# A hybrid recurrent and convolution layer on one core: the order of work in the first chunk of the input projection

## The chip, the cores and the metric

The kernel runs on one core of a Trainium2 chip. The core has TensorE for matmuls (PE in the profile; its weight loads are PEld), VectorE (DVE), ScalarE (ACT), GpSimd (POOL) and SyncE (SP), which issues nearly all transfers here. The metric is the device time of one execution in microseconds (us).

## The reference

One decoder layer over 512 prompt tokens and 8 x 4 sample tokens. A combined projection gives four branches, which are mixed, projected, normalised and sent through a SwiGLU block. Cut to what bears on the change:

```python
z = x @ w_in                       # x: (tokens, 1024), w_in: (1024, 8192)
a_x, a_gate, b_val, b_gate, c_in, d_b, d_c, d_h, gates = jnp.split(z, ...)   # 8 parts of 512 columns, 4 x 1024 gates
a_conv = causal_dwconv(rg_buf, a_x, rg_conv_w)          # width 4, then the RG-LRU recurrence
glu = b_val * jax.nn.sigmoid(b_gate)
b_conv = causal_dwconv(cf_buf, glu, cf_conv_w)          # width 31, then LayerNorm and swish
y_c = pool_mixer(pool_buf, c_in, ...)                   # trailing means over 2/4/8/16 tokens, small matmuls
sc_conv = causal_dwconv(sc_buf, d_c * d_h, sc_conv_w)   # width 3: the "short conv"
y_d = d_b * sc_conv
merged = sum(jax.nn.sigmoid(gates[n]) * (branches[n] @ w_branch[n]))
x = layer_norm(ALPHA * x + merged @ w_out)
x = layer_norm(ALPHA * x + (silu(x @ w_ff_gate) * (x @ w_ff_up)) @ w_ff_down)
```

The outputs are the tokens and the last rows of every convolution buffer. All is float32, to float32 accuracy.

## The kernel before, in words

**Layout.** Activations stand transposed, channels on the 128 partitions and 544 tokens (512 prompt, 32 sample) along the free dimension. Every float32 operand is split into a high and a low part in the 32-bit format that TensorE takes at full rate, and a product is three matmuls: low weights by high x, high by low, high by high.

**Units.** Weights come in units of up to 8 x 128 x 128 elements, through a ring of four slots. For each unit SyncE issues the transfer (`raw`), ScalarE makes the high part (`hi`, line 669, to `w_hi`), GpSimd the low part (`lo`, line 528, to `w_lo`), and TensorE runs `unit` (line 1089): 8 chunks of x, three products, two halves of 272 tokens, so 48 matmuls or 24 pairs.

**The input projection.** It has four chunks of 128 channels (c = 0 to 3), each of 8 units in the order B_VAL, B_GATE, D_C, D_H, D_B, C_IN, A_X, A_GATE. They alternate between two PSUM slots (`main`), and `in_tile` (lines 697 and 1115) couples the engines by counts of emptied slots (`tile_out`). ScalarE empties most units. D_H is emptied by VectorE itself, which multiplies it by d_c into `dch_pad` (lines 1567 to 1570). This is the short-conv product, and unit 5 of a chunk, C_IN, can't start on TensorE before it is done, as both use the same slot.

**VectorE in a chunk** (from line 1548): it waits for `tails_taken`, a transpose of TensorE at the end of the chunk before; builds `glu_pad`; convolves the 32 sample tokens in three instructions (`conformer_steps`, lines 1526 to 1530); adds prompt taps 0 to 11 of the width-31 convolution (`conformer_taps`, line 1545, one instruction a tap); makes the short-conv product and its three taps, taps 12 to 15, y_d, taps 16 to 28, the width-4 convolution, the last taps and their sum (line 1600). In the last chunk `lambda_parts` prepares ScalarE's exp.

**The start.** TensorE transposes x (lines 1099 and 1108), runs unit 0, then transposes small vectors and states that came in 21 small transfers (lines 1126 to 1138, 17 transposes), then runs unit 1, then waits for the copies of these transposes out of PSUM (`misc_ready`, `tails_out`), sends a transpose that counts as `tails_taken` (line 1145), and enters the loop over chunks. ScalarE copies the transposed states (confT, line 686; poolT, line 690), then makes the high parts of units 2 and 3 and of the small matrices (`sm_hi`), then empties units 0 and 1.

**The end of a chunk.** TensorE transposes the last rows of the padded buffers (`turn_tails`, lines 1153 to 1157); some of them are packed by ScalarE first (line 735). In the last chunk this stands in the first group of gate units.

**The order** is the order of the code on each engine. No planner moves it.

Of the kernel before, what the change touches and what calls it, by code (L numbers as in the profile page):

```python
# [70 lines left out]
M_ROWS = V_SCW + SC_TAPS  # L71
CONF_TAPS_1, CONF_TAPS_2, CONF_TAPS_3 = 12, 16, 29

# [30 lines left out]
def build(nc, i_, o_):  # L104
    with ExitStack() as ctx:
# [398 lines left out]
        def _(pool):  # L504
# [26 lines left out]
            for u in range(RING):  # L531
                lo(u, u, 8)
            pool.wait_ge(sm_hi_ready, 1)
            pool.tensor_tensor(sm_lo[:, :, :], sm_raw[:, :, :], sm_hi[:, :, :].bitcast(F32),
                               ALU.subtract).then_inc(sm_lo_ready, 1)
            own = Chain(pool, pool_own)
# [39 lines left out]
            for c in range(KW):  # L576
                for j in range(8):
                    u = RING + 8 * c + j
                    lo(u, u % RING, 8 if u < U_MIX else (8, KW)[u % 2])
                    if j == 5:  # L580
                        window_step(c, 0)
                        if c >= 1:
                            window_step(c, 1)
                    if j == 6:
                        for step in range(2, c + 1):
                            window_step(c, step)
                    if j == 7:
                        window_mean(c)
# [72 lines left out]
        def _(act):  # L661
# [9 lines left out]
            def u_quot(u, s):  # L671
                return (u - s) * (16 // RING) + 16


            act.wait_ge(turned, 1)
            act.activation(x_hi[:, :, SEQ:NT], aux[:, 3, 0:256].rearrange("p (k n) -> p k n", k=KD),
                           ACT.Copy).then_inc(x_hi_ready, 1)
            hi(0, 0)
            for k in range(KD):
                act.wait_ge(turned, k + 2)  # L680
                bank = (main, aux)[k // 4]
                act.activation(x_hi[:, k, 0:SEQ], bank[:, k % 4, :], ACT.Copy).then_inc(x_hi_ready, 1)
            hi(1, 1)
            for g in range(2):
                act.wait_ge(turned, KD + 3 + g)
                act.activation(confT[:, 2 * g:2 * g + 2, :],
                               aux[:, 1 + g, 0:480].rearrange("p (c n) -> p c n", c=2), ACT.Copy)\
                   .then_inc(conf_ready if g == 0 else tile_out[1], 1)
            act.wait_ge(turned, KD + 5)
            act.activation(poolT[:, :, :], aux[:, 3, 0:480].rearrange("p (c n) -> p c n", c=KW), ACT.Copy)\  # L690
               .then_inc(tails_out, 1)
            for u in range(2, RING):
                hi(u, u)
            act.wait_ge(sm_landed, 5 * 16)
            act.activation(sm_hi[:, :, :], sm_raw[:, :, :], ACT.Copy).then_inc(sm_hi_ready, 1)

            def in_tile(idx, c):

# [26 lines left out]
                elif kind == A_GATE:  # L725
                    act.activation(halves(agate[:, c, :]), ps, ACT.Copy).then_inc(out_sem, 1)
                hi(u + RING, idx % RING)

# [27 lines left out]

            for idx in range(2):
                in_tile(idx, 0)
            with act.Fori(0, KW - 1) as c:
# [307 lines left out]
        def _(pe):  # L1067
# [52 lines left out]
            pe.wait_ge(x_lo_ready, 3)  # L1120
            unit(0, 0, x_in, 0, ready=x_lo_ready, n0=1)

            pe.wait_ge(small_landed, 16 * N_SMALL)
            pe.wait_ge(x_lo_ready, KD + 1)
            for c in range(KW):
# [14 lines left out]
            mm.then_inc(turned, 1)  # L1140
            in_tile(1, 0)

# [292 lines left out]
        def _(ve):  # L1435
# [3 lines left out]
            def vec(c, j):  # L1439
                return miscT[:, c, j:j + 1]  # L1440
# [5 lines left out]
            for k in range(KD):  # L1446
# [5 lines left out]
            ve.tensor_copy(miscT[:, :, :], aux[:, 0, 0:KW * M_ROWS].rearrange("p (c n) -> p c n", c=KW))\  # L1452
              .then_inc(misc_ready, 1)
            ve.tensor_copy(lnT[:, :], aux[:, 0, KW * M_ROWS:KW * M_ROWS + 32]).then_inc(tile_out[0], 1)

# [67 lines left out]
            def conformer_steps(c):  # L1523
# [5 lines left out]
                                            axis=mybir.AxisListType.X, op=ALU.add)))  # L1529
                link(ve.tensor_scalar(out, out, vec(c, V_CFB), None, ALU.add))  # L1530

# [16 lines left out]
            for c in range(KW):  # L1548
# [9 lines left out]
                ve.wait_ge(glu_made, c + 2)  # L1558
                conformer_steps(c)
                taps_done = [None, None]  # L1560
                conformer_taps(c, range(0, CONF_TAPS_1), taps_done)

# [12 lines left out]
                            lambda t: vec(c, V_SCW + t), None, st_d)  # L1575
                conformer_taps(c, range(CONF_TAPS_1, CONF_TAPS_2), taps_done)
                ve.wait_ge(tile_out[0], c * 4 + 4)
# [13 lines left out]
                            lambda t: vec(c, V_RGW + t), vec(c, V_RGB), st_a)  # L1591
                after(st_a[1])
                after(link(ve.tensor_copy(Y_A[:, c, :], xc[:, c, :])))
                ve.tensor_tensor(Y_A[:, c + KW, :], xc[:, c, :], Y_A[:, c, :].bitcast(F32), ALU.subtract)\
                  .then_inc(ax_used, 1)
                if c == KW - 1:
                    lambda_parts()
                conformer_taps(c, range(CONF_TAPS_3, CF_TAPS), taps_done)
                after(max(taps_done))
                ve.tensor_tensor(bconv[:, c, 0:SEQ], bconv[:, c, 0:SEQ], aux[:, 3, 0:SEQ], ALU.add)\  # L1600
                  .then_inc(conf_done, 1)
                ve.wait_ge(conf_done, c + 1)
# [444 lines left out]
```

## Time and profile before

| | us |
|---|---|
| median of 3 runs | 987.01 (985.88 to 987.18) |
| the profiled execution | 988.56 |
| its span | 986.8 |
| TensorE busy | 944.2 (96%) |
| TensorE weight loads busy | 936.1 (95%) |
| VectorE busy | 622.5 (63%) |
| GpSimd busy | 383.7 (39%) |
| ScalarE busy | 379.4 (38%) |

The span runs from the first to the last instruction of the profiled execution, and the execution's own time has 1.8 us around it. Busy shares are means over the whole program: a stage can wait for VectorE though that is idle for a third of the span. The granted clock of TensorE, 0.98 on the whole, is read by stretch.

### The profile page before, as it was taken

The numbers are of one execution on the slowest core, as the hardware profiler recorded it, in microseconds if no ns is written. First come the engines' busy times: TensorE is split into PE (matmuls) and PEld (weight loads), VectorE is DVE, ScalarE is ACT, GpSimd is POOL, SyncE is SP. The second block draws the span as 40 slices with busy tenths as digits, with TensorE's granted clock in tenths as the row PEclk, the third lists the DMA queues.
The fourth block names the chain that finished last, engine by engine and source line by source line (L and its number), as shares of the span: only waits on it lengthen the run. The fifth ranks groups of instructions, "written<-read, shape, count | busy, mean of one in ns | idle before, by whom it ended". The sixth has DMA issues, their size and how long they took to land.

```text
span 986.8 us, 18908 instructions
## 1 busy us (share of the span) xinstructions
PE 944.2 (96%) x7382; PEld 936.1 (95%) x7382; DVE 622.5 (63%) x915; ACT 379.4 (38%) x591; POOL 383.7 (39%) x298
## 2 busy tenths in 40 slices
PE   6979999999999999999999988999999999999993
PEld 5979999999999999999999987999999999999993
DVE  2696979795202888453335877988788788321117
ACT  3423232325637323333322345655555547321211
POOL 3736565647364354444445664000000003443423
PEclk9989999999999999999999997999999999999996
DMA  8523232222322332332233211343343343423202
GB/s 234 151 65 95 85 94 85 85 64 76 95 65 66 96 86 76 93 96 86 75 118 107 65 44 43 87 128 85 98 115 85 97 116 98 139 81 88 68 1 91
DMA packets 166658, 89.34 MB, mean 91 GB/s; under 512 B 4635, under 2 KB 164675, under 8 KB 166610
## 3 DMA queue, kind: packets, MB, share of 16 engines
q1 hardware_dynamic: 164377, 87.75, 31.1%
q10 hardware_dynamic: 2232, 0.92, 0.4%
q8 instruction: 34, 0.56, 0.2%
q14 instruction: 15, 0.12, 0.0%
HBM read 85.49 MB, written 3.17 MB: 90 GB/s over the span
## 4 chain that ended last, share of the span: by engine, by line
PE 81%; DVE 10%; POOL 3%; issue 3%; SPq 2%; ACT 1%; DMA 1%; DVEq 0%; POOLq 0%
PE main L1089 51%; PE main L1311 18%; PE main L1239 4%; PE aux L1311 3%; DVE aux L1545 2%; PE aux L1089 2%; POOL x_lo L625 2%; PE aux L1075 1%; SPq L425 1%; DMA ln_tok<-in_ln_b 1%; POOL acc_q L617 1%; POOL wx_lo L606 1%; DVE glu_pad L1556 0%; DVE aux L1526 0%; SPq L393 0%
## 5 line engine op out<-in xcount | busy, mean ns | idle before, releaser
L528 POOL TENSOR_TENSOR w_lo<-raw,w_hi 128x1024 fp32r<-128x1024 f32 (+1 forms) x128 | 280.6, 2196 | 546.4 <-ACT w_hi L669 544.1
L1089 PE MATMUL main<-x_hi,w_lo 128*128 128x272 f32 x1024 | 213.1, 289 | 7.6 <-DVE dch_pad L1570 6.5
L1089 PE MATMUL main<-x_hi,w_hi 128*128 128x272 f32 x1024 | 212.5, 289 | 0.0
L1089 PE MATMUL main<-x_lo,w_hi 128*128 128x272 f32 x1024 | 211.7, 288 | 0.0
L669 ACT ACTIVATE w_hi<-raw 128x1024 fp32r<-128x1024 f32 x128 | 135.0, 1056 | 144.4 <-PE main L1089 139.8
L1089 PEld LDWEIGHTS main<-x_hi,w_lo 128*128 128x128 f32 x1024 | 161.5, 189 | 8.4 <-issue 6.7
L1089 PEld LDWEIGHTS main<-x_lo,w_hi 128*128 128x128 f32 x1024 | 161.3, 189 | 0.0
L1089 PEld LDWEIGHTS main<-x_hi,w_hi 128*128 128x128 f32 x1024 | 160.4, 189 | 0.0
L1089 PE MATMUL main<-y,w_hi 128*128 128x272 f32 x512 | 84.6, 287 | 0.0
L1545 DVE SCALAR_TENSOR_TENSOR aux<-glu_pad,miscT,aux 128x512 f32<-128x512 f32 x112 | 75.2, 748 | 0.0
L1089 PEld LDWEIGHTS main<-y,w_hi 128*128 128x128 f32 x512 | 72.1, 188 | 0.0
L773 ACT ACTIVATE sig<-main 128x544 f32<-128x544 f32 x32 | 20.0, 624 | 131.1 <-PE main L1089 131.1
L1615 DVE TENSOR_TENSOR prod<-main,sig 128x544 f32<-128x544 f32 x24 | 17.4, 724 | 71.5 <-PE main L1089 69.8
L1708 DVE SCALAR_TENSOR_TENSOR scr<-x_lo,main 128x544 f32<-128x544 f32 x6 | 4.3, 721 | 86.8 <-PE main L1089 86.8
L1089 PE MATMUL main<-h_lo,w_hi 128*128 128x272 f32 x264 | 54.6, 288 | 0.0
L1089 PE MATMUL main<-y,w_lo 128*128 128x272 f32 x256 | 53.3, 290 | 1.2 <-DVE prod L1615 1.2
L1311 PE MATMUL main<-x_sum_hi,w_lo 128*128 128x272 f32 x160 | 46.4, 290 | 0.2 <-issue 0.2
L1311 PE MATMUL main<-x_sum_hi,w_sum_lo 128*128 128x272 f32 x160 | 46.2, 289 | 0.1
L1311 PE MATMUL main<-x_sum_hi,w_hi 128*128 128x272 f32 x160 | 46.3, 289 | 0.0
L1311 PE MATMUL main<-x_sum_hi,w_sum_hi 128*128 128x272 f32 x160 | 46.2, 289 | 0.0
L1311 PE MATMUL main<-x_sum_lo,w_hi 128*128 128x272 f32 x160 | 46.1, 288 | 0.0
L1311 PE MATMUL main<-x_sum_lo,w_sum_hi 128*128 128x272 f32 x160 | 46.1, 288 | 0.0
(363 smaller groups left out, 2165.3 us busy)
## 6 DMA issues: line engine op xcount, KB each, us to landing
raw<-in_w_in SPq DMA_DIRECT2D x64, 512.0 KB, 4.1
raw<-in_w_ff_gate SPq DMA_DIRECT2D x22, 512.0 KB, 4.0
raw<-in_w_ff_up SPq DMA_DIRECT2D x22, 512.0 KB, 5.1
raw<-in_w_branch SPq DMA_DIRECT2D x32, 256.0 KB, 3.5
raw<-in_w_ff_down SPq DMA_DIRECT2D x16, 512.0 KB, 3.9
raw<-in_w_out SPq DMA_DIRECT2D x8, 512.0 KB, 3.8
raw<-in_w_ff_down SPq DMA_DIRECT2D x8, 384.0 KB, 3.3
x_tok<-in_x_prompt SPq DMA_DIRECT2D x4, 512.0 KB, 6.4
```

The source lines that it names most:

```text
L425: sp.dma_start(dst, src).then_inc(small_landed, 16)
L528: pool.tensor_tensor(w_lo[s][:, 0:n, :], raw[s][:, 0:n, :], w_hi[s][:, 0:n, :].bitcast(F32), ALU.subtract).then_inc(w_lo_ready, 1)
L606: pool.tensor_tensor(dst[:, :, :], raw[s][:, :, :], src_hi[:, :, :].bitcast(F32), ALU.subtract).then_inc(w_lo_ready, 1)
L617: pool.tensor_tensor(acc_q[:, :], acc_q[:, :], rsq[m % 2][:, :], ALU.add)\
L625: pool.tensor_tensor(x_lo[:, k, cols], merged[:, k, cols], x_hi[:, k, cols].bitcast(F32), ALU.subtract).then_inc(x1_lo_ready, 1)
L669: act.activation(w_hi[s][:, :, :], raw[s][:, :, :], ACT.Copy).then_inc(w_hi_ready, 1)
L773: act.activation(halves(sig[mm][:, :]), slot(0), ACT.Sigmoid).then_inc(tile_out[0], 1)
L1089: mm = pe.matmul(ps[:, h, :], w[s][:, k, :], x[:, h * HALF:(h + 1) * HALF], start=(first and k == 0 and j == 0), stop=(last and k == n - 1 ...
L1239: mm = pe.matmul(bank, w[:, k, :], x[:, cols], start=(first and k == k0 and j == 0), stop=(last and k == k0 + len(xs) - 1 and j == 2))
L1311: mm = pe.matmul(bank, w[:, k0 + k, :], x, start=(first and k == 0 and j == 0), stop=(k == KH - 1 and j == 2), skip_group_check=not first)
L1545: state[t % 2] = link(ve.scalar_tensor_tensor(out, pin, vec(c, V_CFW + t), bank, ALU.mult, ALU.add))
L1615: ve.tensor_tensor(halves(prod[:, :]), slot(1), halves(sig[mm][:, :]), ALU.mult)\
```

## The change

TensorE runs unit 1 directly behind unit 0, and the 17 small transposes come after it. ScalarE then has another order at the start: high parts 1 and 2, empty unit 0 and unit 1, high part 3, the three copies of transposed states, high parts 4 and 5, `sm_hi`. GpSimd's `sm_lo` moves behind the low part of unit 6. On VectorE `conformer_steps` moves in every chunk from the head to the end, and in chunk 0 four taps instead of 12 stand ahead of the short-conv product (12 instead of four behind it). Two waits are added to VectorE, one ahead of the copy to lnT and one on `sm_lo_ready` in chunk 0.

```diff
@@ -69,7 +69,7 @@
-CONF_TAPS_1, CONF_TAPS_2, CONF_TAPS_3 = 12, 16, 29
+CONF_TAPS_0, CONF_TAPS_1, CONF_TAPS_2, CONF_TAPS_3 = 4, 12, 16, 29
@@ -530,9 +530,6 @@
             for u in range(RING):
                 lo(u, u, 8)
-            pool.wait_ge(sm_hi_ready, 1)
-            pool.tensor_tensor(sm_lo[:, :, :], sm_raw[:, :, :], sm_hi[:, :, :].bitcast(F32),
-                               ALU.subtract).then_inc(sm_lo_ready, 1)
@@ -577,6 +574,10 @@
                 for j in range(8):
...
                     lo(u, u % RING, 8 if u < U_MIX else (8, KW)[u % 2])
+                    if c == 0 and j == 2:
+                        pool.wait_ge(sm_hi_ready, 1)
+                        pool.tensor_tensor(sm_lo[:, :, :], sm_raw[:, :, :], sm_hi[:, :, :].bitcast(F32),
+                                           ALU.subtract).then_inc(sm_lo_ready, 1)
                     if j == 5:
@@ -672,29 +673,7 @@
-            act.wait_ge(turned, 1)
...
-            hi(1, 1)
-            for g in range(2):
...
-            for u in range(2, RING):
-                hi(u, u)
-            act.wait_ge(sm_landed, 5 * 16)
-            act.activation(sm_hi[:, :, :], sm_raw[:, :, :], ACT.Copy).then_inc(sm_hi_ready, 1)
-
-            def in_tile(idx, c):
+            def in_tile(idx, c, ahead=True):
@@ -724,7 +703,34 @@
                     act.activation(halves(agate[:, c, :]), ps, ACT.Copy).then_inc(out_sem, 1)
-                hi(u + RING, idx % RING)
+                if ahead:
+                    hi(u + RING, idx % RING)
+
+            act.wait_ge(turned, 1)
...
+            hi(1, 1)
+            hi(2, 2)
+            in_tile(0, 0, ahead=False)
+            in_tile(1, 0, ahead=False)
+            hi(3, 3)
+            for g in range(2):
+                act.wait_ge(turned, KD + 3 + g)
+                act.activation(confT[:, 2 * g:2 * g + 2, :],
+                               aux[:, 1 + g, 0:480].rearrange("p (c n) -> p c n", c=2), ACT.Copy)\
+                   .then_inc(conf_ready if g == 0 else tile_out[1], 1)
+            act.wait_ge(turned, KD + 5)
+            act.activation(poolT[:, :, :], aux[:, 3, 0:480].rearrange("p (c n) -> p c n", c=KW), ACT.Copy)\
+               .then_inc(tails_out, 1)
+            for u in range(RING, RING + 2):
+                hi(u, u % RING)
+            act.wait_ge(sm_landed, 5 * 16)
+            act.activation(sm_hi[:, :, :], sm_raw[:, :, :], ACT.Copy).then_inc(sm_hi_ready, 1)
@@ -754,8 +760,6 @@
-            for idx in range(2):
-                in_tile(idx, 0)
             with act.Fori(0, KW - 1) as c:
                 for idx in range(2, 8):
                     in_tile(idx, c)
@@ -1119,9 +1123,9 @@
             pe.wait_ge(x_lo_ready, 3)
             unit(0, 0, x_in, 0, ready=x_lo_ready, n0=1)
+            unit(1, 1, x_in, 1)
 
             pe.wait_ge(small_landed, 16 * N_SMALL)
-            pe.wait_ge(x_lo_ready, KD + 1)
             for c in range(KW):
                 pe.transpose(aux[:, 0, c * M_ROWS:(c + 1) * M_ROWS], misc_tok[:, c * P:c * P + P],
@@ -1138,7 +1142,6 @@
             mm.then_inc(turned, 1)
-            in_tile(1, 0)
...
             pe.wait_ge(misc_ready, 1)
             pe.wait_ge(tails_out, 1)
@@ -1451,6 +1454,7 @@
             ve.wait_ge(turned, KD + 2)
...
+            ve.wait_ge(tile_out[0], 1)
             ve.tensor_copy(lnT[:, :], aux[:, 0, KW * M_ROWS:KW * M_ROWS + 32]).then_inc(tile_out[0], 1)
@@ -1527,7 +1531,7 @@
-                link(ve.tensor_scalar(out, out, vec(c, V_CFB), None, ALU.add))
+                ve.tensor_scalar(out, out, vec(c, V_CFB), None, ALU.add).then_inc(conf_done, 1)
@@ -1556,9 +1560,9 @@
                 ve.wait_ge(glu_made, c + 2)
-                conformer_steps(c)
                 taps_done = [None, None]
-                conformer_taps(c, range(0, CONF_TAPS_1), taps_done)
+                first = CONF_TAPS_0 if c == 0 else CONF_TAPS_1
+                conformer_taps(c, range(0, first), taps_done)
 
@@ -1573,7 +1577,7 @@
                 st_d = [None, None]
...
-                conformer_taps(c, range(CONF_TAPS_1, CONF_TAPS_2), taps_done)
+                conformer_taps(c, range(first, CONF_TAPS_2), taps_done)
                 ve.wait_ge(tile_out[0], c * 4 + 4)
                 after(st_d[1])
@@ -1590,6 +1594,8 @@
                 after(st_a[1])
+                if c == 0:
+                    ve.wait_ge(sm_lo_ready, 1)
@@ -1597,8 +1603,8 @@
                     lambda_parts()
                 conformer_taps(c, range(CONF_TAPS_3, CF_TAPS), taps_done)
                 after(max(taps_done))
-                ve.tensor_tensor(bconv[:, c, 0:SEQ], bconv[:, c, 0:SEQ], aux[:, 3, 0:SEQ], ALU.add)\
-                  .then_inc(conf_done, 1)
+                after(link(ve.tensor_tensor(bconv[:, c, 0:SEQ], bconv[:, c, 0:SEQ], aux[:, 3, 0:SEQ], ALU.add)))
+                conformer_steps(c)
                 ve.wait_ge(conf_done, c + 1)
             ch.flush()
```

ScalarE at the start, from its high part of unit 1 on; `w_hi_55` to `w_hi_58` are the ring's slots 0 to 3. Before:

```order
L669 ACTIVATE w_hi_56<-raw_52 128x1024
L686 ACTIVATE confT<-aux 128x480 x2
L690 ACTIVATE poolT<-aux 128x480
L669 ACTIVATE w_hi_57<-raw_53 128x1024
L669 ACTIVATE w_hi_58<-raw_54 128x1024
L695 ACTIVATE sm_hi<-sm_raw 128x1536
L706 ACTIVATE b_val<-main 128x544
L669 ACTIVATE w_hi_55<-raw_51 128x1024
L708 ACT_TABLE_LOAD
L708 ACTIVATE b_sig<-main 128x544
```

The same place after:

```order
L670 ACTIVATE w_hi_56<-raw_52 128x1024
L670 ACTIVATE w_hi_57<-raw_53 128x1024
L685 ACTIVATE b_val<-main 128x544
L687 ACT_TABLE_LOAD
L687 ACTIVATE b_sig<-main 128x544
L670 ACTIVATE w_hi_58<-raw_54 128x1024
L724 ACTIVATE confT<-aux 128x480 x2
L728 ACTIVATE poolT<-aux 128x480
L670 ACTIVATE w_hi_55<-raw_51 128x1024
L670 ACTIVATE w_hi_56<-raw_52 128x1024
L733 ACTIVATE sm_hi<-sm_raw 128x1536
```

The three copies now stand behind the emptying of units 0 and 1 and the high part of unit 3.

VectorE in chunk 0, from the head of the chunk to the short-conv product (`dch_pad<-main,d_c`). Before:

```order
L1551 COPY glu_pad<-confT 128x8x30
L1554 TENSOR_TENSOR glu_pad<-b_val,b_sig 128x512
L1556 TENSOR_TENSOR glu_pad<-b_val,b_sig 128x8x4
L1526 TENSOR_TENSOR aux<-glu_pad,miscT 128x992
L1528 TENSOR_REDUCE bconv<-aux 128x32
L1530 TENSOR_SCALAR bconv<-bconv,miscT 128x32
L1537 TENSOR_SCALAR aux<-glu_pad,miscT 128x512
L1541 TENSOR_SCALAR aux<-glu_pad,miscT 128x512
L1545 SCALAR_TENSOR_TENSOR aux<-glu_pad,miscT,aux 128x512 x10
L1563 COPY dch_pad<-miscT 128x8x2
L1567 TENSOR_TENSOR dch_pad<-main,d_c 128x272
```

The same place after:

```order
L1555 COPY glu_pad<-confT 128x8x30
L1558 TENSOR_TENSOR glu_pad<-b_val,b_sig 128x512
L1560 TENSOR_TENSOR glu_pad<-b_val,b_sig 128x8x4
L1541 TENSOR_SCALAR aux<-glu_pad,miscT 128x512
L1545 TENSOR_SCALAR aux<-glu_pad,miscT 128x512
L1549 SCALAR_TENSOR_TENSOR aux<-glu_pad,miscT,aux 128x512 x2
L1567 COPY dch_pad<-miscT 128x8x2
L1571 TENSOR_TENSOR dch_pad<-main,d_c 128x272
```

Eleven instructions ahead of the product, three of the sample sum and eight taps, are now behind it.

## Rows read from the trace of the kernel before

**Rows 1.** The waits of TensorE: total us, times, longest us.
```profile
PE main L1089 <- DVE dch_pad L1570: 6.5, 1, 6.5
...
PE aux L1126 <- DMA ln_tok<-in_ln_b: 2.0, 1, 2.0
...
PE aux L1156 <- ACT packed L735: 0.7, 1, 0.7
```

**Rows 2.** TensorE in order of time: start, us, what ran.
```profile
20.49 0.41 PE L1089 MATMUL main<-x_hi,w_hi 128*128 128x272 f32 x2
22.86 0.84 PE L1126 MATMUL aux<-ident,misc_tok 94*128 94x94 f32 x4 [1.95 <-DMA ln_tok<-in_ln_b]
...
26.39 0.52 PE L1089 MATMUL main<-x_hi,w_lo 128*128 128x272 f32 x2
...
32.55 0.49 PE L1089 MATMUL main<-x_hi,w_lo 128*128 128x272 f32 x2
...
50.42 0.41 PE L1089 MATMUL main<-x_hi,w_hi 128*128 128x272 f32 x2
57.34 0.82 PE L1089 MATMUL main<-x_hi,w_lo 128*128 128x272 f32 x2 [6.51 <-DVE dch_pad L1570]
...
64.86 0.41 PE L1089 MATMUL main<-x_hi,w_lo 128*128 128x272 f32 x2
...
234.20 0.54 PE L1156 MATMUL aux<-ident,packed 128*120 128x128 f32 x3 [0.71 <-ACT packed L735]
```

**Rows 3.** Busy time by stretch, then granted clock, DMA share, GB/s.
```profile
13.50:14.00 0.50, 0.00 (x0) 0.00 (x0) 0.50 (x2) 0.50 (x2) 0.00 (x0) 1.00 0.72 168
...
24.00:25.00 1.00, 1.00 (x6) 1.00 (x7) 0.63 (x2) 0.03 (x1) 0.00 (x0) 0.50 0.82 238
...
59.00:60.00 1.00, 1.00 (x7) 1.00 (x6) 1.00 (x3) 0.00 (x0) 0.00 (x0) 0.50 0.00 0
```

**Rows 4.** VectorE in order of time, chunk 0, and one row of chunk 3.
```profile
32.93 3.57 DVE L1551 COPY glu_pad<-confT 128x240 f32<-128x240 f32 x1 [8.30 <-PE aux L1145]
...
41.65 3.33 DVE L1526 TENSOR_TENSOR aux<-glu_pad,miscT 128x992 f32<-128x992 f32 x1
...
46.24 2.19 DVE L1530 TENSOR_SCALAR bconv<-bconv,miscT 128x32 f32<-128x32 f32 x1
...
49.71 6.67 DVE L1545 SCALAR_TENSOR_TENSOR aux<-glu_pad,miscT,aux 128x512 f32<-128x512 f32 x10
...
57.03 0.18 DVE L1570 TENSOR_TENSOR dch_pad<-main,d_c 128x32 f32<-128x32 f32 x1
...
191.26 1.20 DVE L1526 TENSOR_TENSOR aux<-glu_pad,miscT 128x992 f32<-128x992 f32 x1
```

**Rows 5.** GpSimd in order of time.
```profile
17.68 2.39 POOL L528 TENSOR_TENSOR w_lo<-raw,w_hi 128x1024 fp32r<-128x1024 f32 x1 [8.59 <-ACT w_hi L669]
...
231.82 0.25 POOL L567 TENSOR_TENSOR win<-win,cin_pad 128x32 f32<-128x32 f32 x1
```

**Rows 6.** The chain that ended last: start, us, what.
```profile
187.07 0.44 PE aux L1153 x4
...
233.34 0.82 ACT packed L735 x4
```

**Rows 7.** ScalarE in order of time.
```profile
26.55 0.57 ACT L690 ACTIVATE poolT<-aux 128x480 f32<-128x480 f32 x1 [0.21 <-PE aux L1138]
27.02 2.00 ACT L669 ACTIVATE w_hi<-raw 128x1024 fp32r<-128x1024 f32 x2
...
231.87 0.63 ACT L773 ACTIVATE sig<-main 128x544 f32<-128x544 f32 x1
```

**Rows 8.** Transfers issued between 17 and 18 us: KB each, us to landing.
```profile
raw<-in_w_in SPq DMA_DIRECT2D x1, 512.0 KB, 6.2
```

**Rows 9.** The waits of VectorE up to 240 us.
```profile
DVE glu_pad L1551 <- PE aux L1157: 19.5, 3, 8.5
...
DVE merged L1612 <- PE aux L1157: 2.4, 1, 2.4
```

More of the change, by code:

```diff
@@ L672, in u_quot @@
                 return (u - s) * (16 // RING) + 16
-            act.wait_ge(turned, 1)
[L676 to L682, printed above, removed]
-            hi(1, 1)
-            for g in range(2):
[L685 to L691, printed above, removed]
-            for u in range(2, RING):
-                hi(u, u)
-            act.wait_ge(sm_landed, 5 * 16)
-            act.activation(sm_hi[:, :, :], sm_raw[:, :, :], ACT.Copy).then_inc(sm_hi_ready, 1)
-            def in_tile(idx, c):
+            def in_tile(idx, c, ahead=True):
                 kind = IN_ORDER[idx]
@@ L726, in in_tile @@
                     act.activation(halves(agate[:, c, :]), ps, ACT.Copy).then_inc(out_sem, 1)
-                hi(u + RING, idx % RING)
+                if ahead:
+                    hi(u + RING, idx % RING)
+            act.wait_ge(turned, 1)
+            act.activation(x_hi[:, :, SEQ:NT], aux[:, 3, 0:256].rearrange("p (k n) -> p k n", k=KD),
+                           ACT.Copy).then_inc(x_hi_ready, 1)
+            hi(0, 0)
+            for k in range(KD):
+                act.wait_ge(turned, k + 2)
+                bank = (main, aux)[k // 4]
+                act.activation(x_hi[:, k, 0:SEQ], bank[:, k % 4, :], ACT.Copy).then_inc(x_hi_ready, 1)
+            hi(1, 1)
[15 more added lines that the diff above has]
+            act.activation(sm_hi[:, :, :], sm_raw[:, :, :], ACT.Copy).then_inc(sm_hi_ready, 1)
             def pack_tails(c):
```

## The prediction

> **What bounds the kernel.** I read the table of waits first. The first short-conv product holds TensorE for 6.5 us, the small input DMAs for 2.0 and a ScalarE copy for 0.7 [rows 1]; of these three the diff touches every one. TensorE otherwise runs its matmul pairs 0.25 us apart nearly to the end of the span, so a microsecond taken out of its own row of work should be a microsecond of the span, unless a later wait takes it back.
>
> TensorE's timeline gives each wait its place. Unit 0's last pair starts at 20.49, the small transposes only at 22.86 (the vectors have not landed), unit 1 at 26.39, unit 2 at 32.55. Units 2, 3 and 4 then run without a hole; their last pair starts at 50.42 and unit 5 at 57.34 [rows 2]. The stretches show the clock: it is at its lower level (1.2 GHz) in 24 to 25 and 59 to 60, behind the idle stretches from 20.9 and 50.8, and at the upper (2.4 GHz) in 13.5 to 14, an idle piece inside a gap of 1.13 us [rows 3].
>
> VectorE is why unit 5 waits. Its chunk starts at 32.93. The sample filter sum of chunk 0 (product, reduction, bias) takes 41.65 to 48.43, ten taps 6.67, and only at 57.2 is the short-conv product done [rows 4]. TensorE needed it at 50.67.
>
> **Part 1: unit 1 ahead of the transposes.** Before, unit 2 starts at 32.55. After: unit 1 can start at 20.49 + 0.25 = 20.74, since its low parts are ready at 17.68 + 2.39 = 20.07 [rows 5] and its bank is free by unit 0's own waits on x_lo. 24 pairs of 0.25 make 6.02: 26.76. The small vectors landed by 22.8, under unit 1, so the 2.0 wait is gone. The 17 small transposes took 22.86 to 26.39 = 3.53, at the lower clock. At the upper clock four transposes take 0.44 in a later chunk, 0.11 each [rows 6], so 17 take 1.87 and end at 28.63. Both ends: 1.87 and 3.53. I take 1.87, because now a whole unit runs right ahead of them, as eight do ahead of the 0.44.
>
> The change adds a wait here. Before, unit 1 covered the ScalarE copies of the transposed states; now TensorE stands behind them (tails_out), and ScalarE has its own queue ahead: the sigmoid of unit 1, the high part of unit 3, then three copies. From unit 1's end at about 26.92 that is 0.63 + 1.00 + 3 x 0.57 = 3.34 us [rows 7], to 30.26. The sigmoid's table load comes before the wait for unit 1 and is covered by it. Unit 3's weights, issued between 17 and 18 and landed 6.2 us later [rows 8], at about 24.1, are there by 27.5. What queues behind the waiting transpose is all of TensorE, so unit 2 starts at 30.3. Gain: 32.55 - 30.3 = 2.25. With slow transposes they end at 30.29, the last copy 0.57 later, and unit 2 starts near 31.0: 1.55. If the copies overlap as before (26.55 to 27.02 between two starts [rows 7]), unit 2 starts at 29.9: 2.65.
>
> **Part 2: the product of chunk 0 comes earlier.** Ahead of the product go away the filter sum, 48.43 - 41.65 = 6.78, and eight taps, 8 x 0.667 = 5.3. Together 12.1 us, and the chunk starts 2.3 us earlier: the product would end at 57.2 - 14.4 = 42.8. It can't be that early, because it reads unit 3's bank, complete at 30.3 + 2 x 6.02 = 42.35; the product's three instructions take some 0.9 (57.2 less the end of the taps and the pad copy, [rows 4]), so 43.3. Unit 5 needs it at 30.3 + 18.1 = 48.4. Cover: 5 us. The hole between unit 4 and unit 5, 57.34 - 50.67 = 6.67, closes. Behind it goes the slow clock: unit 5 ran from 57.34 to 64.86 (the pair at which unit 6 begins) = 7.52 [rows 2] against 6.02, so 1.50 more. This could be less only if the clock had another reason to fall.
>
> **Part 3: the filter sum at the end of every chunk.** The same three instructions run, so VectorE's total does not change. In chunks 0 to 2 they fall in front of a VectorE wait for the tail transposes (8.5 us the longest of three, 19.5 together) [rows 9]. In chunk 3 they leave the head, where they took 2.65 (1.20 + 1.19 + 0.24, no GpSimd beside them; the first is in [rows 4]), and TensorE's tail transposes come out: there TensorE waited 0.71 for ScalarE's packing, which stood behind lambda_parts, exp, a table load and a sigmoid that began at 231.87 although its matmuls were long done [rows 1, 7]. With VectorE 2.65 earlier, exp and table load are over before the gate unit ends; packing then waits for GpSimd, whose last window instruction ends at 231.82 + 0.25 = 232.07 [rows 5], and its four copies take 0.82 [rows 6]: 232.9, ahead of the 233.5 at which TensorE was ready (234.20 less 0.71, [rows 2]). Gain 0.71; bounds 0 (GpSimd later by 0.5) and 0.71. Behind it, the sum in chunk 3 runs until the next VectorE work, which waited 2.4 us [rows 9], so it is covered.
>
> The first of these instructions took 3.33 us in chunk 0 and 1.20 in chunk 3 [rows 4]; in chunk 0 GpSimd was running low parts all the while. The Trainium skill (GPSIMD Engine Reference, Specifications) says that GpSimd's SBUF interface is shared with VectorE and that VectorE contends in a 2-port mode or with two SBUF inputs. The trace agrees, with 3.33 against 1.20. That speaks against the change: the sum's new place is beside GpSimd's window means. By it each of the sum's two SBUF-bound instructions may take some 2 us more, up to 6.8 instead of 2.65; by the undisturbed row 2.65. Either way the wait behind it covers it in chunks 1 to 3; in chunk 0, VectorE may reach chunk 1 late by up to 2 us, where it has the 2.65 taken out of the head and spare time before the product, so the sum is the same by both.
>
> **Part 4: the rest.** sm_lo (3.5 us on GpSimd) moves from behind four low parts to behind three more. Its first reader, the side matmuls, runs 200 us later. Unit 7's low part goes behind it and is ready at about 46.2, needed at 60.4. High parts 4 and 5 move behind poolT, ready by 32.3 and 36 with their low parts, needed at 42.3 and 48.4. GpSimd's part for unit 2 is early (22.5 instead of 30.5), so the DMA for unit 6 starts earlier; no one waits for it. The added waits of lnT's copy and of xc's copy are on counts long reached. All of it at 0; if any cover were missing, it would be the low part of unit 5, with 12 us to spare.
>
> **Sum.** 2.25 + 6.67 + 1.50 + 0.71 = 11.13. The profiled execution took 988.56 (span 986.8 and 1.8 around it): 977.4. It lies 1.55 above the median of the runs, 987.01, and I take the same gain from that: 975.9.
>
> **Rivals.**
> A, the clock falls in the new gap. TensorE is now idle from 28.6 to 30.3, 1.7 us. For: idle from 20.9 to 22.86, 1.95 us, the clock fell. Against: a gap of 1.13 at 13.5 left it up [rows 3]. 1.7 is nearer the first, but the stretch in front is fuller. Price: a unit slow as unit 5 was, 1.5: 977.4.
> B, the transposes stay slow at 3.53 though nothing is idle ahead: 0.7 less gained, 976.6.
> C, the wait comes back on VectorE: GpSimd blocks the glu copies, the tap's pad copy and the product in chunk 0 (the first took 3.57 beside sm_lo [rows 4]). Four such instructions at 3.5, four taps at 0.7 and the product's 0.9 would end it at 48.0, just before 48.4. Past that, every microsecond costs itself, and up to 1.5 for the clock. With 2 us late: 979.4.
> D, slower than before. The new queue in front of TensorE decides it: unit 3's weights stand ahead of the copies that release it. Unit 2 starts at their landing + 1.00 + 1.71, if that is later than 30.3. The whole gain of 11.1 is spent when they land at 38.7 instead of 24.1; at 40 the time is 988.3. The rows speak against it: 14.6 us more on a transfer of 6.2 [rows 8].
> E, the change does not take hold: the filter sum and taps are off the path, but unit 5 waits as long for something else, ScalarE's copy of unit 3 or 4. These follow a unit by 0.6 us in the trace. Only 2.25 + 0.71 gained: 984.0.
>
> **Chances.** Forecast 0.58, A 0.22, B 0.07, C 0.06, E 0.03, D 0.01; 0.03 for gains unseen, of which the clock after later waits is the likeliest (it was low in other places, and where it falls can shift by a microsecond or two). The range for 8 in 10: down by 0.4 for the overlapping copies and 2 for the clock elsewhere, 973.5; up over A with 2 beside it, 979.5. Differences under 0.2%, 2 us, can't be told from none. Faster than 985.0: all but D and a part of E and of the rest, 0.96; same 0.02; slower 0.02.
>
> **What would show it.** TensorE's waits: no line for the small DMAs, none for dch_pad, none for packed; a new one of 1.4 to 1.7 for poolT's copy near 28.6. Unit 2 at 30.3, unit 5 at 48.4 and unit 6 at 54.4, clock at the upper level from 15 to 80. The 17 transposes within 2 us. VectorE waits for TensorE ahead of the product of chunk 0; its wait at the head of chunk 1 shrinks from 8.5 to nearly nothing. Wrong if unit 5 starts after 49, if pairs after 30 us stand over 0.3 apart, or if TensorE shows a wait over 2 us in the chunks that it did not have.

## The result, and the profile after

| | before | changed |
|---|---|---|
| median of runs (lowest to highest) | 986.44 us (985.24 to 987.18) | 976.69 us (976.55 to 978.20) |
| changed / before | | 0.9908, 95% interval 0.9893 to 0.9922 |
| profiled execution, span | 988.56, 986.8 | 976.55, 974.8 |

The change makes the kernel 9.75 us faster by the medians. The forecast was 975.9 in a range of 973.5 to 979.5, a gain of 11.1: the time lies in the range, and 0.8 above the forecast.

The page's row of busy time for each engine, first after:

```profile
PE 939.2 (96%) x7382; PEld 931.7 (96%) x7382; DVE 633.9 (65%) x915; ACT 379.5 (39%) x591; POOL 390.4 (40%) x298
```

and of the kernel before:

```profile
PE 944.2 (96%) x7382; PEld 936.1 (95%) x7382; DVE 622.5 (63%) x915; ACT 379.4 (38%) x591; POOL 383.7 (39%) x298
```

The counts are equal, so nothing was taken out of the work. VectorE is busy 11.4 us longer with the same 915 instructions. The rows below show why for some of them: they run beside GpSimd and are done only once its instruction has ended. No wait of TensorE shows this, but it matters below.

The largest waits of TensorE after, and the one of the last chunk (total us, times, longest us), to be held against [rows 1]:

```profile
PE main L1242 <- POOL x_lo L626: 5.9, 4, 2.7
PE aux L1103 <- DMA xs_tok<-in_x_sample: 3.4, 1, 3.4
PE main L1112 <- DMA x_tok<-in_x_prompt: 3.0, 1, 3.0
PE aux L1433 <- DVE scr L1975: 2.2, 1, 2.2
PE main L1242 <- POOL wx_lo L607: 1.3, 3, 0.8
PE aux L1148 <- ACT poolT L728: 1.3, 1, 1.3
...
PE aux L1159 <- ACT packed L741: 0.7, 1, 0.7
```

The 6.5 us for dch_pad and the 2.0 for the small DMAs are gone. The copy of poolT is the new wait, as forecast. The wait for packed stands where it stood.

TensorE in order of time after (start, us, what ran), against [rows 2]:

```profile
25.72 0.42 PE L1093 MATMUL main<-x_hi,w_hi 128*128 128x272 f32 x2
25.97 0.49 PE L1130 MATMUL aux<-ident,misc_tok 94*128 94x94 f32 x4
...
27.44 0.57 PE L1142 MATMUL aux<-ident,pool_tok 120*128 120x120 f32 x4
29.27 0.30 PE L1148 MATMUL aux<-ident 128*128 128x128 f32 x1 [1.26 <-ACT poolT L728]
29.62 0.51 PE L1093 MATMUL main<-x_hi,w_lo 128*128 128x272 f32 x2
...
47.51 0.41 PE L1093 MATMUL main<-x_hi,w_hi 128*128 128x272 f32 x2
47.76 0.41 PE L1093 MATMUL main<-x_hi,w_lo 128*128 128x272 f32 x2
...
223.14 0.54 PE L1159 MATMUL aux<-ident,packed 128*120 128x128 f32 x3 [0.74 <-ACT packed L741]
```

The transposes follow unit 1's last pair at the pair distance of 0.25, TensorE stands still for 1.26 us, and unit 2 starts at 29.62. Unit 5 starts at 47.76, 0.25 behind the last pair of unit 4; before there were 6.9 us between the two. And the stretches (busy time of each engine, then granted clock, DMA share, GB/s), against [rows 3]:

```profile
28.00:29.00 1.00, 0.01 (x1) 0.00 (x0) 0.00 (x0) 1.00 (x4) 1.00 (x1) 1.00 1.18 294
...
50.00:60.00 10.00, 10.00 (x82) 10.00 (x81) 9.93 (x13) 1.71 (x5) 6.26 (x4) 1.00 0.21 59
```

The clock is at its upper level through the new gap and through unit 5, and stays there up to 573 us.

**Where the time went.** The profiled executions differ by 12.0 us, more than the medians. Unit 0 starts at 13.85 instead of 14.61, which the change can't have done: 0.76 of luck. From unit 0 to unit 2 it is 17.94 before and 15.77 after: 2.17. From unit 2 to ScalarE's emptying of unit 5 (start of its copy, 65.06 before, 53.97 after) it is 32.51 and 24.35: 8.16. That is 11.09 by the end of unit 5. Some 0.9 more is gained behind it: 0.66 near 613 us of the kernel before and 0.36 near 971, both in or beside stretches with the clock at its lower level, behind waits that both kernels have. The two steps alone make 10.33, near the 9.75 of the medians.

### The profile page after: what moved, and what is told of

Read it like the earlier page. It is cut to its first block, busy times and chain, and to the rows that moved or that the text cites. A ratio compares the mean times of both kernels' runs of the same rounds, so it can differ in the third digit from the quotient of the medians.

```text
span 974.8 us, 18907 instructions
## 1 busy us (share of the span) xinstructions
PE 939.2 (96%) x7382; PEld 931.7 (96%) x7382; DVE 633.9 (65%) x915; ACT 379.5 (39%) x591; POOL 390.4 (40%) x298
## 4 chain that ended last, share of the span: by engine, by line
PE 86%; DVE 7%; POOL 3%; issue 2%; ACT 1%; DMA 1%; SPq 0%; DVEq 0%; POOLq 0%
PE main L1093 55%; PE main L1314 18%; PE main L1242 4%; PE aux L1314 3%; PE aux L1093 2%; POOL x_lo L626 2%; DVE aux L1549 1%; PE aux L1079 1%; DMA x_tok<-in_x_prompt 1%; POOL wx_lo L607 1%; POOL acc_q L618 0%; DVE scr L1633 0%; PE aux L1382 0%; POOL w_lo L528 0%; DVE xc L1506 0%
```

## The experiments

All were timed in five rounds against the kernel before, in three sets of kernels. Of before the medians in them were 987.14, 986.07 and 985.70. A gain in us below is the difference of two medians. The ratio beside it is taken from all runs and mostly gives a little less (0.9909, for one, is 9.0 us where the medians give 10.0), and its interval reaches 1.3 to 2.4 us to each side. Where two kernels of one set differ by less than that, the trace has to show the term.

**The start alone.** The changed kernel, with VectorE's order put back to that of before. The transposes, the copies and also GpSimd's `sm_lo` stay moved:

```
+CONF_TAPS_0, CONF_TAPS_1, ... = 12, 12, 16, 29
 ve.wait_ge(glu_made, c + 2)
+conformer_steps(c)              # at the chunk's head, as before
```

> The new order at the start alone (TensorE, ScalarE, GpSimd); VectorE keeps the sample filter sum at the head of each chunk and 12 taps ahead of the short-conv product. Theory (the parts add): unit 2 starts 2.2 us earlier than before, VectorE starts its chunk as much earlier, the product ends near 54 us, unit 5 waits about 6.3 us for it and then runs 1.5 us at the lower clock: 2.2 us faster than before, 984.2. Rival (the parts cover each other: without VectorE's part an earlier unit 2 only lengthens the wait for the product, since GpSimd's operations then hold VectorE longer): under 1 us faster.

Measured: 978.77 us, ratio 0.9922 (0.9898 to 0.9945), 8.4 faster. Both theories fail: a change that was worth 2.2 us gives nearly the whole. TensorE still waits for the product of chunk 0, but for 1.0 us and not 6.5:

```profile
PE main L1093 <- DVE dch_pad L1575: 1.0, 1, 1.0
```

VectorE's rows of chunk 0 (start, us) show why:

```profile
30.74 0.62 DVE L1555 COPY glu_pad<-confT 128x240 f32<-128x240 f32 x1 [2.38 <-PE aux L1148]
...
36.52 1.20 DVE L1530 TENSOR_TENSOR aux<-glu_pad,miscT 128x992 f32<-128x992 f32 x1
...
49.62 0.18 DVE L1575 TENSOR_TENSOR dch_pad<-main,d_c 128x32 f32<-128x32 f32 x1
```

The same instructions, head of the chunk to product, take 19.1 us here (30.74 to 49.80) and 24.3 before (32.93 to 57.21) [rows 4]. The sum's first took 3.33 there and 1.20 here. The difference stands on GpSimd. Its rows before:

```profile
28.15 4.75 POOL L528 TENSOR_TENSOR w_lo<-raw,w_hi 128x1024 fp32r<-128x1024 f32 x2 [8.08 <-ACT w_hi L669]
32.84 3.52 POOL L534 TENSOR_TENSOR sm_lo<-sm_raw,sm_hi 128x1536 fp32r<-128x1536 f32 x1
36.31 7.61 POOL L528 TENSOR_TENSOR w_lo<-raw,w_hi 128x1024 fp32r<-128x1024 f32 x3
46.00 2.39 POOL L528 TENSOR_TENSOR w_lo<-raw,w_hi 128x1024 fp32r<-128x1024 f32 x1 [2.08 <-ACT w_hi L669]
```

and in this kernel:

```profile
28.86 7.57 POOL L528 TENSOR_TENSOR w_lo<-raw,w_hi 128x1024 fp32r<-128x1024 f32 x3 [6.16 <-ACT w_hi L670]
38.59 2.38 POOL L528 TENSOR_TENSOR w_lo<-raw,w_hi 128x1024 fp32r<-128x1024 f32 x1 [2.16 <-ACT w_hi L670]
40.93 3.52 POOL L579 TENSOR_TENSOR sm_lo<-sm_raw,sm_hi 128x1536 fp32r<-128x1536 f32 x1
```

Before, GpSimd ran without a pause from 28.15 to 43.9, and VectorE's glu copy, its two glu products and the sum's first instruction were each done only once a piece of GpSimd's had ended. With sm_lo's 3.52 us moved back GpSimd is still from 36.4 to 38.6, and the sum's first instruction goes through. Of the 5.2 us, 2.95 are the glu copy (0.62 instead of 3.57) and 2.13 the sum's first. Its bias addition is held in both kernels (2.04 and 2.19). The part whose cost I had put at nothing was a suspect.

**VectorE's order alone.** The kernel before, with the sum behind the taps and four taps ahead of the product; the start and GpSimd, `sm_lo` too, are as before:

```
+first = CONF_TAPS_0 if c == 0 else CONF_TAPS_1      # 4, 12
-conformer_steps(c)              # now behind the chunk's taps
```

> VectorE's part alone: the sample filter sum behind the last taps, four taps ahead of the product in chunk 0; the start as before. Theory: the wait of 6.5 us and the 1.5 us of low clock behind it go, the start keeps its 2.0 us wait and its slow transposes: 8.2 us faster, 978.2. Rival (something else holds unit 5 once VectorE is early): a wait of TensorE over 1 us at unit 5 in the profile and a gain under 6.

Measured: 979.27 us, 0.9923 (0.9898 to 0.9948), 7.9 faster. Unit 5 waits for nothing. It is VectorE that waits at the product, for unit 3:

```profile
45.11 0.44 DVE L1567 TENSOR_TENSOR dch_pad<-main,d_c 128x272 f32<-128x272 f32 x1 [1.66 <-PE main L1089]
```

The start keeps its wait and the slow stretch behind it (waits, then 25 to 26 us with the clock at 0.50):

```profile
PE aux L1126 <- DMA ln_tok<-in_ln_b: 2.6, 1, 2.6
```

```profile
25.00:26.00 1.00, 1.00 (x5) 0.69 (x4) 0.00 (x0) 0.85 (x3) 0.00 (x0) 0.50 0.85 235
```

The theory holds: 7.9 where 8.2 was expected. But 8.4 and 7.9 alone, against 10.0 together (below), means that the parts overlap: each closes most of the same wait.

**All twelve taps ahead of the product.** The rest is the changed kernel.

```
-CONF_TAPS_0, ... = 4, ...
+CONF_TAPS_0, ... = 12, ...
```

> The changed kernel with 12 taps, not four, ahead of the product in chunk 0. Theory (moving the filter sum was enough): VectorE ends its taps near 43.5, is held by GpSimd's low part until about 46, and ends the product near 46.9, 0.8 us before TensorE needs it at 47.75: no wait at unit 5, the time of the changed kernel within 0.5 us. Rival (the four taps are needed): the product is late by 1 to 3 us, unit 5 waits and runs slowly behind it, 2 to 4 us slower than the changed kernel.

Measured: 977.23 us, 0.9904 (0.9880 to 0.9928), the changed kernel's own time. The product ends at 47.3, ahead of unit 5's need, though GpSimd held the tap's pad copy for most of its 2.38:

```profile
44.16 2.38 DVE L1567 COPY dch_pad<-miscT 128x16 f32<-128x16 f32 x1
...
47.12 0.17 DVE L1574 TENSOR_TENSOR dch_pad<-main,d_c 128x32 f32<-128x32 f32 x1
```

So the theory holds: with the rest of the change in place, four taps instead of 12 bring nothing that can be measured.

**The change once more**, in the same rounds:

> The changed kernel once more, timed in the same rounds as its parts. Theory: 10.3 us faster than before, the sum of the terms that its trace shows (2.2 at the start, 8.1 at unit 5, nothing in the last chunk): 976.2. Rival (the measured 9.75 is the true gain, because some executions of before lose less to the low clock than the profiled one): 9.0 to 9.9 faster.

Measured: 977.17 us, 0.9909 (0.9885 to 0.9933), 10.0 faster. That is between the two expectations, 10.3 and 9.0 to 9.9, and the interval can't tell them apart.

**sm_lo alone.** The kernel before, with one GpSimd instruction moved behind the low parts of units 4 to 6, and a wait of VectorE on a count long reached:

```
-pool.wait_ge(sm_hi_ready, 1)
-pool.tensor_tensor(sm_lo[...], sm_raw[...], sm_hi[...], ALU.subtract)
 lo(u, u % RING, ...)
+if c == 0 and j == 2: # the same two statements here
```

> The kernel before with one instruction moved: GpSimd's sm_lo (3.5 us) behind the low part of unit 6. VectorE's order, TensorE's and ScalarE's are those of before. Theory (in chunk 0 VectorE is held by GpSimd's row of operations, which sm_lo makes unbroken from 32.8 to 43.9): without it VectorE's glu copies and filter sum are held 4 to 6 us less, the product ends at 51 to 53 instead of 57.2, unit 5 waits 0 to 2 us and the clock stays up: 6 to 8 us faster than before, 979 to 981. Rival (the filter sum and the taps in front of the product are the cost, as the prediction had it): unit 5 still waits over 4 us and the gain is under 3.

Measured: 980.16 us, 0.9945 (0.9926 to 0.9963), 5.9 faster. The rows are like those of the first experiment: the sum's first instruction again takes 1.20, the product ends at 51.9, TensorE waits 1.0.

```profile
38.42 1.20 DVE L1527 TENSOR_TENSOR aux<-glu_pad,miscT 128x992 f32<-128x992 f32 x1
...
51.74 0.17 DVE L1571 TENSOR_TENSOR dch_pad<-main,d_c 128x32 f32<-128x32 f32 x1
```

The glu copy takes 2.34 instead of 3.57, the small glu product 0.18 instead of 2.39 and the sum's first 1.20 instead of 3.33. Together that is 5.6 us, and the product comes 5.3 earlier. A move to which no wait of TensorE points gives some three fifths of the gain of all moves, because it shortens a conflict between two engines neither of which bounds the kernel.

The experiments now add up: the start without `sm_lo` was forecast at 2.2, and 2.2 with `sm_lo`'s 5.9 is 8.1 (8.4 measured), with VectorE's 7.9 it is 10.1 (10.0 measured). What overlaps is `sm_lo` and VectorE's order, not the start.

**Four taps alone.** The kernel before, and in it nothing else than

```
+first = CONF_TAPS_0 if c == 0 else CONF_TAPS_1      # 4, 12
-conformer_taps(c, range(0, CONF_TAPS_1), taps_done)
+conformer_taps(c, range(0, first), taps_done)
```

> The kernel before with four instead of 12 taps ahead of the product in chunk 0, nothing else. Theory: the product ends 5.3 us earlier, at 51.9; unit 5 waits 1.2 us and the clock stays up as it does in other gaps of that size: 5.4 + 1.5 = 6.9 us faster than before, 980.2. Rival (GpSimd's operations hold what now comes earlier): the wait stays over 3 us and the gain under 5.

Measured: 979.85 us, 0.9947 (0.9926 to 0.9967), 6.2 faster, with a wide spread: ten of the 12 runs lie between 977.84 and 982.09, two at 985.6 and 985.96, where the kernel before lies. In the profile the product ends at 49.7 and unit 5 waits for nothing, where 1.2 us had been expected. The product comes 7.5 us earlier, and eight taps are only 5.3 of that. Most of the rest is the sum's bias addition:

```profile
45.95 0.24 DVE L1530 TENSOR_SCALAR bconv<-bconv,miscT 128x32 f32<-128x32 f32 x1
```

It starts 0.27 us ahead of GpSimd's next low part (46.22) here and takes 0.24; before, it started 0.24 behind it (46.24 and 46.00) and took 2.19. That is how two instructions happen to meet, and no work of the taps. The eight taps, without effect behind the rest of the change, are worth up to 6 us without it.

**The sum back at the head of chunks 1 to 3:**

```
 ve.wait_ge(glu_made, c + 2)
+if c > 0: conformer_steps(c)
```

> The changed kernel, with the filter sum behind the taps in chunk 0 alone and at the head again in chunks 1 to 3. Theory (in those chunks VectorE's lead is used up by holds of GpSimd, so the move brings nothing): within 0.5 us of the changed kernel, and lambda_parts in chunk 3 comes 42.3 us after the chunk's start, as in both. Rival (the lead helps somewhere later): 0.7 to 2 us slower than the changed kernel, or a new wait for the product in chunk 1.

Measured: 977.52 us, 0.9920 (0.9896 to 0.9943). The changed kernel was not in these rounds; in others it took 976.69 to 978.23, so no difference is shown. The wait for packed is 0.7 in both. In chunks 1 to 3 no gain of the sum's move is shown, and the step on the last chunk can't rest on it.

**Lambda's parts ahead of the thirteen middle taps** of the last chunk:

```
+if c == KW - 1: lambda_parts()
 conformer_taps(c, range(CONF_TAPS_2, CONF_TAPS_3), taps_done)
 ...
-if c == KW - 1: lambda_parts()
```

> The changed kernel with lambda_parts of the last chunk ahead of taps 16 to 28. Theory: ScalarE's exp and both table loads are done long before the gate unit ends, packing waits for GpSimd's window alone (end at 221.0), and TensorE's wait of 0.74 us for the packed rows goes: 0.7 us faster than the changed kernel in the profile. Rival (GpSimd or ax_used is as late): the wait stays above 0.4.

Measured: 976.28 us, 0.9906 (0.9883 to 0.9929), 1.2 less than the kernel of the experiment before in the same rounds (the ranges overlap: 975.53 to 977.48 and 976.39 to 979.00). The wait is gone. ScalarE after, first in the changed kernel:

```profile
219.29 0.21 ACT L827 ACTIVATE spv<-spv 128x4 f32<-128x4 f32 x1 [3.44 <-DVE spv L1467]
219.51 1.28 ACT L777 ACT_TABLE_LOAD   x1
220.81 0.62 ACT L777 ACTIVATE sig<-main 128x544 f32<-128x544 f32 x1
...
222.28 0.39 ACT L741 ACTIVATE packed<-glu_pad 128x240 f32<-128x240 f32 x1
```

then in this one:

```profile
216.61 0.20 ACT L827 ACTIVATE spv<-spv 128x4 f32<-128x4 f32 x1
...
221.79 0.41 ACT L741 ACTIVATE packed<-glu_pad 128x240 f32<-128x240 f32 x1 [0.48 <-POOL win L564]
```

and TensorE, without an idle time in brackets:

```profile
222.98 0.49 PE L1159 MATMUL aux<-ident,packed 128*120 128x128 f32 x3
```

The exp on spv no longer holds up the sigmoid, and packing now waits for GpSimd's windows, as the forecast had it. From the emptying of unit 5 to the last tail transposes it is 0.96 shorter than in the changed kernel (168.59 against 169.55).

**The copies ahead of unit 3's high part**, to shorten the new wait:

```
 in_tile(1, 0, ahead=False)
-hi(3, 3)
 ...                              # confT, poolT
+hi(3, 3)
```

> The changed kernel with ScalarE's high part of unit 3 behind the three copies that TensorE waits for, not ahead of them. Theory (ScalarE's queue sets the new wait): the idle time between the small transposes and unit 2 falls from 1.3 us to 0.3, unit 2 starts 1.0 us earlier, unit 3's parts are still ready by 32 against 35: 1.0 us faster than the changed kernel. Rival (the wait ends with something else, or VectorE, held by GpSimd's later row, is late at the product): no gain, or a wait at unit 5.

Measured: 977.10 us, 0.9913 (0.9891 to 0.9936), 1.1 less than the changed kernel in the same rounds. The wait shrinks only from 1.26 to 0.86, since ScalarE then waits for the transposes themselves:

```profile
27.74 1.03 ACT L723 ACTIVATE confT<-aux 128x480 f32<-128x480 f32 x2 [0.43 <-PE aux L1137]
```

So 0.4 is shown by the trace, where 1.0 was expected; the rest of the 1.1 is within what the rounds leave open.

**The copies last**, behind the high parts of units 3 to 5, to make the new wait long enough to see its price:

```
 in_tile(1, 0, ahead=False)
-hi(3, 3)
+for u in range(3, RING + 2): hi(u, u % RING)
 ...                              # confT, poolT
-for u in range(RING, RING + 2): hi(u, u % RING)
```

> The changed kernel with ScalarE's high parts of units 3, 4 and 5 all ahead of the copies, so that TensorE's new wait grows from 1.3 to some 3.3 us. Theory (rival A of the prediction at a longer gap): 2.0 us for the wait, and the clock falls behind it, 1.5 more: 3.5 us slower than the changed kernel. Rival (the clock stays up): 2.0 slower, all matmul pairs of unit 2 at 0.25 us.

Measured: 981.38 us, 0.9960 (0.9947 to 0.9973), 3.15 more than the changed kernel in the same rounds. The wait is 3.9 us, and the clock behind it low:

```profile
PE aux L1147 <- ACT poolT L729: 3.9, 1, 3.9
```

```profile
33.00:34.00 1.00, 1.00 (x7) 1.00 (x6) 1.00 (x1) 0.38 (x1) 1.00 (x1) 0.50 0.95 287
```

From unit 0's start to the emptying of unit 5 it is 5.2 longer: 2.65 of wait and some 2.55 of clock. About 1 of it comes back near 600 us, the rest of the difference to 3.15 I can't place. So rival A's mechanism is real at a gap of 3.9; its price there is higher than my 1.5, and the gap is longer than the one that this change makes.

**Both improvements together**, lambda early and the copies first:

> The changed kernel with the copies first and lambda_parts early, as in the two runs on each. Theory (the two gains add): 1.0 + 0.7 = 1.7 us faster than the changed kernel, about 975.1, and faster than both. Rival (the time moves by what the clock does in the waits behind the projection, and hides them): within 0.5 of the changed kernel.

Measured: 975.93 us, 0.9899 (0.9878 to 0.9921): the lowest median of all. The two gains add, as the theory had it (1.7 expected): it lies 2.3 under

**the change a third time**, the control of these rounds:

> The changed kernel once more, in the same rounds as the three others, so that differences of a microsecond are taken between runs of one chip. Expected at 976.2 to 977.2; its profile within 1 us of the first in the start of unit 2.

Measured: 978.23 us, 0.9926 (0.9904 to 0.9949), a microsecond above what was expected; unit 2 starts at 30.11, within 0.5 us of the first profile. The changed kernel's three medians, 976.69, 977.17 and 978.23, spread by 1.5, so a difference of a microsecond is taken only between kernels of one set.

## Why the prediction was right, and where not

**Part 1, the start: right.** Forecast 2.25, seen 2.17 (15.77 against 17.94 from unit 0). The transposes took 2.04 us (25.97 to 28.01) where I took 1.87. The wait is 1.26 instead of 1.7: the transposes end later, and ScalarE's three copies take 1.48 us in all (27.64 to 29.12) instead of 1.71, since they overlap as they did before. On the other side unit 2 starts 0.35 behind the transpose that waited, for which I had next to nothing. These small errors cancel. Unit 2 at 29.62 is 0.7 earlier than said, about unit 0's luck.

**Part 2, unit 5: the size right, the reason incomplete.** The hole and the slow unit were put at 8.17 and 8.16 came. The product was said to end at 43.3, limited by unit 3; it ends at 42.87. I put the whole gain down to twelve microseconds of VectorE work taken out ahead of the product, and that alone is enough: with VectorE's two moves and `sm_lo` where it was, unit 5 waits for nothing. So as a term of this sum "all of it at 0" of part 4 stands. What it misses is that VectorE's work was not the only way to the gain. sm_lo's move gives 5.9 alone, four taps 6.2 alone, both VectorE moves 7.9, the start with sm_lo 8.4, and all of it 10.0: several covers for one wait, any one of which nearly closes it. A reader of the forecast would have put sm_lo's move alone at nothing. I had priced it by its reader 200 us later and not by what it does to its neighbours, while the 3.57 and 3.33 in [rows 4] showed the conflict. I used them only as a price of the sum in its new place. The clock's part held: no wait, no slow unit. Not run were the whole change without sm_lo's move, and the sum's move alone.

**Part 3, the last chunk: failed.** This is the term of the sum that did not come. Forecast 0.71, seen 0 (0.74 of wait instead of 0.71); the bound of 0 was named, with another cause. "With VectorE 2.65 earlier" did not come about. TensorE's tail transposes ahead of the chunk end at 187.94 before and 176.85 after; the product starts 15.55 us behind them before and 12.15 after. That lead of 3.4 is the sum's 2.65 taken out of the head, and a pad copy of dch_pad that takes 0.17 instead of 1.75, less 0.42 by which the chunk starts later and a wait of 0.26 for unit 3. But spv comes 42.2 us behind them in both. VectorE lost the lead on the way, each time beside a GpSimd instruction. VectorE after:

```profile
189.00 0.44 DVE L1571 TENSOR_TENSOR dch_pad<-main,d_c 128x272 f32<-128x272 f32 x1 [0.26 <-PE main L1093]
...
190.29 2.38 DVE L1498 TENSOR_SCALAR acc<-dch_pad,miscT 128x32 f32<-128x32 f32 x1
...
196.87 2.69 DVE L1583 TENSOR_TENSOR acc<-acc,d_b 128x544 f32<-128x544 f32 x1
...
219.09 0.16 DVE L1467 TENSOR_TENSOR spv<-miscT,spv 128x4 f32<-128x4 f32 x1
```

and the same two instructions before:

```profile
204.77 0.23 DVE L1494 TENSOR_SCALAR acc<-dch_pad,miscT 128x32 f32<-128x32 f32 x1
...
209.20 1.47 DVE L1579 TENSOR_TENSOR acc<-acc,d_b 128x544 f32<-128x544 f32 x1
```

0.23 became 2.38 and 1.47 became 2.69: 3.4 us, the whole lead. GpSimd's rows after cover the same time:

```profile
190.06 2.56 POOL L528 TENSOR_TENSOR w_lo<-raw,w_hi 128x1024 fp32r<-128x1024 f32 x1 [2.20 <-ACT w_hi L670]
...
196.59 2.39 POOL L528 TENSOR_TENSOR w_lo<-raw,w_hi 128x1024 fp32r<-128x1024 f32 x1 [3.96 <-ACT w_hi L670]
```

The first instruction ends at 192.67, GpSimd's at 192.62; the second ends at 199.56, 0.6 behind GpSimd's 198.98, about what it takes by itself (0.71 in chunk 0). GpSimd's pieces are timed by TensorE's units, so an instruction of VectorE that comes earlier falls under another of them. The experiments agree: with the sum at the head the wait is the same 0.7, and with lambda 13 taps earlier it is gone. That the holds themselves cause it, apart from their matching times, no run isolates in this chunk.

**Part 4.** No wait of TensorE shows a cost of the low parts, the DMAs or the added counts; sm_lo is spoken of above.

**Rivals.** A did not occur: the clock stayed up over 1.26 us. B is out, the transposes took the upper clock. C occurred in part and was harmless. VectorE in chunk 0 after:

```profile
33.06 2.37 DVE L1560 TENSOR_TENSOR glu_pad<-b_val,b_sig 128x32 f32<-128x32 f32 x1
...
42.02 0.44 DVE L1571 TENSOR_TENSOR dch_pad<-main,d_c 128x272 f32<-128x272 f32 x1 [2.01 <-PE main L1093]
...
78.33 2.71 DVE L1530 TENSOR_TENSOR aux<-glu_pad,miscT 128x992 f32<-128x992 f32 x1
```

The glu instructions are held (this one is 2.37 for 32 elements a partition), and VectorE still waits 2.01 for unit 3. The sum's first instruction in its new place takes 2.71 instead of 1.20 and the bias addition 1.02 instead of 0.24, so VectorE starts chunk 1 some 4.4 us after the tail transposes let it, where I had said up to 2; that does not reach TensorE. The wait of 8.5 at that head is gone, as said. D and E did not occur.

**What stays open.** All the runs of the kernel before spread over 8.8 us (980.7 to 989.5), those of the changed one over 3 (976.3 to 979.4). A kernel that depends on how the instructions of two engines meet might vary more (the bias addition of the four-taps run is such a case), but no profile of a run at its lower end was taken. The start differs too: unit 0 starts between 13.6 and 15.2 in all these kernels. TensorE's groups of four transposes of x first follow each other 0.85 us apart and then 0.44. The quick ones begin at 10.7 us after the change and at 12.9 before, with a granted clock of 1.00 in the record throughout, and nothing here tells why.

## What to carry to other kernels

An instruction off the critical path is priced by who runs beside it, not only by who reads it: look for rows of one kind whose duration varies (here 1.20 and 3.33), find the engine whose instruction ends as they end, and try moving that one first. When several edits cover one wait, their gains don't add; time each alone before keeping all. A short prerequisite of another engine's late chain (lambda here) is put far ahead of it, since a lead of a few microseconds gained upstream can be lost before it gets there.

## What the runs showed of the hardware

- Even tiny VectorE instructions can be held while GpSimd works on SBUF. The 128x32 tap took 2.38 instead of 0.23 and ended at 192.67, GpSimd's instruction at 192.62; the 128x32 glu product of chunk 0 took 2.37 after the change and ended at 35.43, GpSimd's row at 35.39; the pad copy of 128x16 elements took 2.38 with 12 taps ahead of the product and ended at 46.54, GpSimd's at 46.50. The taps of 128x512 beside them, which add to a sum in PSUM and write it there, kept their 0.667. The Trainium skill (GPSIMD Engine Reference, Specifications) names the shared interface and when VectorE contends for it. The glu product and the sum's first instruction have two inputs in SBUF, and for them the trace agrees with its rule; the tap and the copy have one, and no trace shows the mode that they ran in. What the trace adds is the price: up to the whole remaining length of the GpSimd instruction.
- TensorE idle for 1.26 us kept the upper clock; behind 1.95 (before) and 3.9 (copies last) it was at the lower. The slow stretch behind 3.9 us cost some 2.55 more. The length of the gap alone does not decide it: near the end both kernels wait 2.22 us for VectorE's `scr`; before, the clock was at 0.50 behind that wait (972 to 974 us) and two transposes took 0.69, after the change it was at 1.00 (960 to 962 us) and the same two took 0.44.
